# Moving the last product of a 16x16 block solve three slots later in a hand-woven RWKV-7 kernel

## The reference, cut to what matters

```
def step(S, inp):
    r_t, w_t, k_t, v_t, a_t, b_t = inp
    sa = jnp.einsum('bhvk,bhk->bhv', S, a_t)
    S = S * w_t[:, :, None, :] + sa[..., :, None] * b_t[..., None, :] + v_t[..., :, None] * k_t[..., None, :]
    y = jnp.einsum('bhvk,bhk->bhv', S, r_t)
    return S, y
```

## Time and profile before

| what | value |
|---|---|
| median of 3 runs | 3546.62 us (3546.22 to 3547.91) |
| profiled execution, its own time | 3549.15 us |
| its span, first to last instruction | 3547.4 us |
| PE busy | 3373.3 us (95%) |
| mean granted PE clock | 0.972 |
| span of rounds 2 to 8 (139.9 to 555.0 us) | 415.1 us |
| PE busy and granted clock, 0 to 625 us | 531.07 us, 0.90 |
| PE busy and granted clock, 625 to 3547.4 us | 2842.19 us, 0.99 |

### The profile page before, as it was taken

One profiled execution on the slowest core, in us unless ns is written; L12 is line 12 of the kernel. 1 busy time (PEld: TensorE's weight loads), 2 busy tenths in 40 slices (PEclk: granted clock), 3 DMA queues, 4 the chain that ended last, 5 costly groups with the idle time before them and its releaser, 6 DMA issues.

```text
span 3547.4 us, 51081 instructions
## 1 busy us (share of the span) xinstructions
PE 3373.3 (95%) x22310; PEld 2185.0 (62%) x22310; DVE 1557.7 (44%) x2977; ACT 751.6 (21%) x1564; POOL 353.1 (10%) x282
## 2 busy tenths in 40 slices
PE   8988887999999999999999899999999999899999
PEld 3455555788884657788886466656445655534344
DVE  4555554788743215687832444454212204201011
ACT  2323232211003024311002223223222320211111
POOL 0011010233001000122100111003000001100000
PEclk9998997999999999999999999999999999899999
DMA  5321202255651220156522110100121114599997
GB/s 196 119 72 45 83 8 73 84 178 178 195 161 60 72 83 1 48 167 190 177 75 72 48 37 25 37 25 2 51 66 48 48 37 155 221 422 421 421 421 285
DMA packets 355791, 452.81 MB, mean 128 GB/s; under 512 B 25712, under 2 KB 282992, under 8 KB 331760
## 3 DMA queue, kind: packets, MB, share of 16 engines
q1 hardware_dynamic: 355568, 449.55, 36.9%
HBM read 445.27 MB, written 4.20 MB: 127 GB/s over the span
## 4 chain that ended last, share of the span: by engine, by line
PE 87%; DVE 6%; DMA 3%; ACT 2%; issue 1%; POOL 1%; SPq 0%; POOLq 0%; DVEq 0%; ACTq 0%
PE bank L79 86%; DMA A<-in_w_up 2%; DVE A L70 2%; DVE A L76 1%; ACT A L87 1%; DMA W<-in_w_up 1%; PE bank L82 1%; DVE SM L76 0%; DVE H L70 0%; DVE A L73 0%; DMA W<-in_mod_w 0%; POOL A L73 0%; ACT SM L87 0%; DVE X L76 0%; DMA A<-in_x 0%
## 5 line engine op out<-in xcount | busy, mean ns | idle before, releaser
L79 PE MATMUL bank<-A 64*64 64x64 f32 (+6 forms) x11424 | 1013.9, 274 | 84.4 <-ACT A L87 32.7
L79 PEld LDWEIGHTS bank<-A 64*64 64x64 f32 (+3 forms) x11424 | 797.6, 154 | 348.5 <-issue 127.8
L79 PE MATMUL bank<-A,W 128*128 128x256 f32 (+1 forms) x2240 | 724.5, 478 | 8.4 <-DMA W<-in_rw_g 7.1
L79 PE MATMUL bank<-H,W 128*128 128x512 f32 (+2 forms) x1712 | 639.5, 523 | 18.6 <-ACT H L87 14.4
L79 PEld LDWEIGHTS bank<-A,W 128*128 128x128 f32 x2240 | 420.5, 192 | 262.9 <-issue 215.9
L87 ACT ACTIVATE A<-bank 128x512 f32<-128x512 f32 (+4 forms) x493 | 208.5, 427 | 1499.3 <-PE bank L79 1455.4
L79 PEld LDWEIGHTS bank<-H,W 128*128 128x128 f32 (+1 forms) x1712 | 313.9, 191 | 276.8 <-issue 245.4
L79 PE MATMUL bank<-A,H 128*64 128x512 f32 (+2 forms) x1224 | 309.6, 572 | 6.2 <-DMA A<-in_w_up 3.4
L70 DVE TENSOR_TENSOR A<-bank,A 128x256 f32<-128x256 f32 (+1 forms) x350 | 157.9, 462 | 179.0 <-PE bank L79 158.1
L79 PEld LDWEIGHTS bank<-A,H 128*64 128x64 f32 (+1 forms) x1224 | 114.0, 145 | 171.8 <-issue 150.7
L70 POOL TENSOR_TENSOR A<-A 128x512 f32<-128x512 f32 (+1 forms) x103 | 146.0, 1425 | 732.6 <-ACT A L87 372.4
(11 more groups left out here) (185 smaller groups left out, 2538.4 us busy)
## 6 DMA issues: line engine op xcount, KB each, us to landing
A<-in_w_gate SPq DMA_DIRECT2D x47, 1024.0 KB, 22.6
W<-in_mod_w SPq DMA_DIRECT2D x45, 1024.0 KB, 7.3
A<-in_w_up SPq DMA_DIRECT2D x42, 1024.0 KB, 19.2
A<-in_w_down SPq DMA_DIRECT2D x35, 1024.0 KB, 27.0
W<-in_mlp_up SPq DMA_DIRECT2D x64, 512.0 KB, 5.4
W<-in_mlp_down SPq DMA_DIRECT2D x128, 256.0 KB, 4.0
W<-in_w_mod SPq DMA_DIRECT2D x24, 1024.0 KB, 5.9
W<-in_w_up SPq DMA_DIRECT2D x22, 1024.0 KB, 18.9
```

The lines of the kernel that those rows point to most:

```text
L79: return self.e.matmul(o, l, r, start=start, stop=stop, skip_group_check=True)
```

## The change

Five things are done, all in the scores stage. GpSimd's spread becomes one `tensor_tensor` of 128x512 that multiplies XI, read twice, by both mask columns, in place of two `tensor_scalar` of 128x256; it and ACT's two spread activations move from slot 11 to slot 14. DVE's `solve16` steps are spread over slots 2 to 13 and the transposes move from slot 12 to 15. Levels 4 and 5 move three slots later on all engines (PE's `u`, `t`/`tt`, `u`, `tt` to slots 16, 18, 19 and 21). The mask of the second `sk` product on DVE moves from slot 6 to slot 5. The `turn` products stay in slots 7, 10 and 13. What each operation computes is unchanged.

```
+        def spread16(e, st, x, rows=slice(0, P)):
+            n = rows.stop - rows.start
+            mask = C("iota")[rows, 68:70].unsqueeze(1).unsqueeze(3).broadcast_to([n, 16, 2, 16])
+            return e.tt(st.rearrange("p (c q j) -> p c q j", q=2, j=16), x.unsqueeze(2).broadcast_to([n, 16, 2, 16]), mask, MUL)
...
 def pe_scores
-            for lev in range(1, 6):
...
+            yield
+            yield
+            for lev in range(4, 6):
+                x, y = (5, 4) if lev % 2 else (4, 5)
+                if lev == 4:
+                    pe.wait_ge(s_gp, ngp["m", ct])
+                    pe.wait_ge(s_dv, ndv["t", ct, 3])
+                else:
+                    pe.wait_ge(s_ac, nac["t", ct, 4])
+                each(x, m8, T_).then_inc(s_pe, npe("u", ct, lev))
+                yield
+                yield
+                pe.wait_ge(s_dv, ndv["tt", ct, lev - 1])
+                pe.wait_ge(s_dv, ndv["a", ct, lev])
                 if lev == 4:
                     each(y, TT, A_).then_inc(s_pe, npe("t", ct, lev))
+                each(x, A_, TT).then_inc(s_pe, npe("tt", ct, lev))
+                yield
 def gp_scores
-            yield from idle(4)
+            yield from idle(7)
             gp.wait_ge(s_dv, ndv["inv", ct])
-            for n in range(2):
-                gp.ts(of16(AM)[:, :, 16 * n:16 * n + 16], XI, parity(n), None, MUL, None).then_inc(s_gp, ngp() if n == 0 else ngp("ett", ct))
-            yield from idle(13)
+            spread16(gp, AM, XI).then_inc(s_gp, ngp("ett", ct))
+            yield from idle(10)
 def ac_scores
+            for n, (dst, b) in enumerate(((Vts[ct % 2], 2), (KHts[ct % 2], 2), (BHts[ct % 2], 3))):
+                yield
+                yield
+                ac.wait_ge(s_pe, npe["tok", ct, n])
+                ac.act(dst, bank8(b), COPY).then_inc(s_ac, nac("tok", ct, n))
+                yield
+            ac.wait_ge(s_dv, ndv["inv", ct])
+            for n in range(2):
+                m = ac.act(of16(TTf)[:, :, 16 * n:16 * n + 16], XI.rearrange("p i c -> p c i"), COPY, scale=parity(n))
+                m.then_inc(s_ac, nac() if n == 0 else nac("et", ct))
             yield from idle(4)
+            ac.wait_ge(s_pe, npe["t", ct, 4])
+            ac.act(T_, bank8(5), COPY).then_inc(s_ac, nac("t", ct, 4))
+            yield from idle(6)
 def dv_scores
-                if j in (2, 3, 4, 6, 7, 9, 11, 13):
+                if j not in (1, 8, 12):
                     yield
                 if j == 2:
                     masked("sk", AKs[ct % 2], 2, 0)
-                if j == 6:
+                if j == 4:
                     masked("sk", AKs[ct % 2], 2, 1)
```

More of the change, by code:

```diff
@@ L1023, in pe_scores @@
             yield
-            for lev in range(1, 6):
-                x, y = (5, 4) if lev % 2 else (4, 5)
+            for n, (src, b) in enumerate(((V, 2), (c8(KH), 2), (c8(BH), 3))):
+                yield
+                yield
+                pe.wait_ge(*((s_gp, ngp["end", ct, n - 1]) if n else (s_ac, nac["v", ct])))
+                pe.wait_ge(*left[b])
+                turn(src, b).then_inc(s_pe, npe("tok", ct, n))
+                left[b] = (s_ac, nac["tok", ct, n])
+                yield
+            yield
+            yield
+            for lev in range(4, 6):
+                x, y = (5, 4) if lev % 2 else (4, 5)
+                if lev == 4:
[4 more added lines that the diff above has]
+                each(x, m8, T_).then_inc(s_pe, npe("u", ct, lev))
                 yield
-                if lev > 3:
-                    pe.wait_ge(s_dv, ndv["tt", ct, lev - 1])
-                    pe.wait_ge(s_dv, ndv["a", ct, lev])
+                yield
+                pe.wait_ge(s_dv, ndv["tt", ct, lev - 1])
+                pe.wait_ge(s_dv, ndv["a", ct, lev])
                 if lev == 4:
                     each(y, TT, A_).then_inc(s_pe, npe("t", ct, lev))
-                if lev > 3:
-                    each(x, A_, TT).then_inc(s_pe, npe("tt", ct, lev))
+                each(x, A_, TT).then_inc(s_pe, npe("tt", ct, lev))
                 yield
[L1035 to L1048, removed]
-            yield from idle(4)
+            yield from idle(2)
         def gp_scores(gp, ct):
@@ L1073, in ac_scores @@
                 ac.wait_ge(s_pe, npe["headed", ct - 2])
[L1074 to L1079, removed]
+            for n, (dst, b) in enumerate(((Vts[ct % 2], 2), (KHts[ct % 2], 2), (BHts[ct % 2], 3))):
                 yield
-                if lev == 4:
-                    ac.wait_ge(s_pe, npe["t", ct, lev])
-                    ac.act(T_, bank8(4 if lev % 2 else 5), COPY).then_inc(s_ac, nac("t", ct, lev))
                 yield
[L1085 to L1088, removed]
+                ac.wait_ge(s_pe, npe["tok", ct, n])
+                ac.act(dst, bank8(b), COPY).then_inc(s_ac, nac("tok", ct, n))
                 yield
+            ac.wait_ge(s_dv, ndv["inv", ct])
+            for n in range(2):
+                m = ac.act(of16(TTf)[:, :, 16 * n:16 * n + 16], XI.rearrange("p i c -> p c i"), COPY, scale=parity(n))
+                m.then_inc(s_ac, nac() if n == 0 else nac("et", ct))
             yield from idle(4)
+            ac.wait_ge(s_pe, npe["t", ct, 4])
+            ac.act(T_, bank8(5), COPY).then_inc(s_ac, nac("t", ct, 4))
+            yield from idle(6)
         def dv_scores(dv, ct):
```

## The result

| | median us | runs | against before |
|---|---|---|---|
| before | 3547.26 (3546.22 to 3549.74) | 4 | |
| changed kernel | 3499.36 (3495.19 to 3502.49) | 4 | 0.9863 [0.9846, 0.9880] |
| changed kernel, run again | 3498.20 (3491.36 to 3503.93) | 4 | 0.9861 [0.9847, 0.9874] |

The change is faster by 48.6 us (1 - 0.9863, of 3547), where 36.5 were forecast. The median lies at the fast edge of the range, and the ratio applied to 3546.62 gives 3498, just outside it.

What follows compares the result with a forecast made beforehand. PE bounds the kernel, idling 4.35 us a round for DVE's transpose, with slow clock added. Savings of 19.2 + 5.5 + 5.0 + 4.3 + 0.5 + 2 = 36.5 us give 3510 us, range 3499 to 3526 (8 in 10).

Steps and rivals of the forecast that it cites:

- the ring: Before u of level 4, PE waits on DVE, DVE on POOL's spread, queued behind a key product awaiting PE: 4.35 us idle.
- queue for the first transpose: DVE operations ahead of the moved transposes: first transpose done 4.8 to 7.3 us after tok 2, 6.3 taken.
- remaining wait: PE at u of level 4, slot 16, still waiting for DVE's transpose: 0.5 us in each full round.
- part (3): End of tok 2 to next score products in a full round: 26.0 us becomes 21.2, 4.8 saved.
- the round ends: Score products behind the chain's last chunk, at 0.56 of clock: 7 us won if clock holds, 2 counted.
- half of the low-clock cost: Between tok 2 and next score products in full rounds: 1.0 of the 2.0 us lost to low clock stays.
- rival D: Clock stays full throughout, all low-clock parts go: 49 us faster, 3498; chance 0.17.
- terms for round 2: 4.35 + 2.0 of clock + 1.3 less 1.4 less 0.8, given as about 5.0 us saved.
- The mask slot: DVE's sk mask from slot 6 to 5: PE's mask wait, 2.16 us in round 8, goes; 2.0 counted there.
- The spread's 0.6 a round: One POOL operation of 1.2 us replaces the pair of 1.82 behind the key product: 0.6 us saved.
- DVE waited for the modulation weights: Later modulation DMA makes DVE wait 1.5 to 2.5 us in slot 1 of rounds 5 to 7; 0 counted for PE.
- Rival C: Levels 4 and 5 in the chain's tail find no cover and half clock: 20 us slower, 3566; chance 0.03.

Runs made afterwards that it cites:

- key_behind: Kernel before with GpSimd's key product one slot later (11 instead of 10), behind the spread; levels 4 and 5 in old slots: 3507.81 us, 0.9890.
- fill_stall: Kernel before with 17 idle 128x128 matmuls on PE between tok 2 and u of level 4, inside the 4.35 us stall: 3544.06 us, 0.9989.
- fill_gate_wait: Changed kernel with 7 idle 128x128 matmuls on PE before the gate product in rounds 4 to 7, inside the rw_g weight wait: 3494.95 us, 0.9853.
- mask_back: Changed kernel with DVE's mask of the second sk product back behind the next slot's solve steps (j = 6 instead of 4): 3509.95 us, 0.9892.
- spread_only: Kernel before with only the single GpSimd spread of 128x512, in slot 11: 3540.32 us, 0.9980.
- two_spreads: Changed kernel with GpSimd's spread as two tensor_scalar of 128x256 again, in slot 14: 3498.82 us, 0.9859.
- key_gate_on_before: Kernel before with the key product behind the spread and the gate product two slots later, levels in old slots: 3495.52 us, 0.9851.
- gate_late_key_behind: Changed kernel with gate product and its DVE use two slots later, and GpSimd's key product behind the spread (slot 14): 3476.99 us, 0.9805.

## Why the prediction was right in its mechanism and off in its size

**Right: the ring.** The wait of the transpose went from 30.4 to 4.9 us, and key_behind shows by another cut that it was order alone. The prediction's queue for the first transpose (4.8 to 7.3 us after tok 2, 6.3 taken) measured 6.1 in round 5. Its remaining wait, put at 0.5 a full round, was 0.9 in rounds 4 and 7, where PE's cover ran at full clock, and 0 in rounds 5 and 6, where it was slower. Round 8 kept 1.8, below the 2 to 3.5 announced. Counted over rounds 2 to 8, PE's idle time fell by 30.4, where the forecast's terms other than clock come to about 27.

**Off: the clock terms.** The step that failed is the size put on the clock in part (3) and at the round ends. The forecast kept half of the low-clock cost in each full round, so it won 1.0 in each of four; it had 2.0 for round 2, about 1.7 for round 3 (5.5 less the stall of 4.35 with its 0.5 of wait left) and 2 of a possible 7 us for the round ends: some 10 us. Measured is 19.0 of PE busy time, of which 7.6 at the ends. By rounds:

| round | forecast less | measured less | of it PE busy |
|---|---|---|---|
| 2 | 5.0 | 6.4 | 3.0 |
| 3 | 5.5 | 8.2 | 3.1 |
| 4, 5, 6, 7 | 4.8 each | 8.5, 6.4, 6.0, 8.6 | 4.4, 1.5, 1.2, 4.4 |
| 8 | 4.3 | 5.2 | 1.3 |
| round ends | 2 | in the rows above | |
| 9 to 11 | 0.5 | 0.8 more | 0.4 less |

Two statements of the prediction failed. "If the denser last chunk keeps the clock, 6 x 1.2 = 7 are won; I count 2": the score products behind round 5 took 1.92 in place of 3.26, and over the six ends from round 3 to round 8 their rows sum to 12.1 us, where they were 19.7: 7.6 us. And "plus half of the low-clock cost" in full rounds: two of four had none (clock 1.00, 56.27 and 56.26 us) and two kept nearly all of it (0.94). Without the round ends PE busy time fell by 3.1, 0.2, 0.2 and 3.1 us in rounds 4 to 7, 1.6 on average against the 1.0 counted, and in no single round by the half. The whole had its own case, rival D (3498, everything at full clock), at 0.17. The result has D's figure without being all of D: two rounds still lose clock, and the waits that remain are smaller than D's 6 us. The experiments separate the two parts: fill_stall gains 13 us in the profiled rounds with the stall in place, and fill_gate_wait brings the last two rounds to 1.00. Two sums of the forecast are loose besides: its terms for round 2 add up to 5.45, not 5.0, and half of 1.8 in round 8 is 0.9, not 1.3.

**Smaller terms.** The mask slot was priced well as a wait: 4.6 us came back in mask_back, against 4.3 forecast; its medians say 10, which is open. The spread's 0.6 a round was 0.8 (spread_only), and nothing once covered. DVE waited for the modulation weights by 1.3, 1.7 and 0.6 us, where 1.5 to 2.5 were announced, and PE didn't notice, as said. Rival C, the uncovered tail, came true only in round 2 (0.8 for the last copy). That levels in the tail keep the clock at the round ends is shown by the table under key_behind (11.9 and 12.1 us with them, 19.0 without, the ring open in all three); mask_back and two_spreads, with the levels moved too, also have 1.92 from the end of round 4 on. It is not the only way: with the gate wait gone as well, key_gate_on_before has full rounds at 1.00 with the levels in their old place.

## What to carry to other kernels

When an engine stands idle behind a queue, ask whether the wait is work or a ring of order: here GpSimd's product waited for TensorE's last instruction while TensorE waited for what GpSimd had queued behind it, and one slot on one engine opened it. Price a removed stall with its clock: PE busy time of the same matmuls, before and after, is the measure, and here it was two fifths of the gain. Then look at what lowers the clock next; the 1.8 us wait for a weight cost more than its own length, and taking it out by two slots gave another 22 us (14.3 of them in the four rounds that had the wait).

## What the runs showed of the hardware

Executions of one kernel differ here by up to 15 us of 3500 (gate_late_key_behind, 3471.80 to 3486.70) though no instruction differs, and within one execution equal rounds differ by whether the granted clock falls to 0.50 (1.2 GHz) behind a 1.8 us wait: 56.3 against 58.5 us. Idle matmuls in that wait narrowed four executions to 1.4 us. GpSimd's tensor_tensor of 128x512 with both inputs broadcast takes 1.04 us alone and 1.48 beside DVE; DVE's operations with two SBUF inputs take up to 1.0 us longer beside GpSimd's products (1.76 against 0.75). A stall of 4.35 us lowers the clock behind it by itself: with the gate wait gone, 52 matmuls behind it took 3.04 us where they take 1.73 behind the filled stall.
